# Other banks in the conv and pool stage, norm sums in mid-unit, and earlier splits of three weight units

## The chip, the cores and the metric

The kernel runs on one core of a Trainium2 chip. The metric is the device time of one execution in microseconds. A core has TensorE (matrix products, fp32 sums into eight PSUM banks), VectorE (DVE), ScalarE (ACT), GpSimd (POOL) and SyncE (SP), which issues the loads. The engines run their own instruction lists and meet only at semaphores.

## The reference

Two transformer-like blocks over 512 tokens of width 1024, all in fp32. The part around the change is the end of the first block (its feed-forward part between two RMS norms) and the first mixer of the second block, which runs a causal convolution of 31 taps on half of the channels and window means on the other half:

```
def hybrid_layer(x, ...):
    ...
    x = x + rms_norm(mix, g_post_mix)                     # norm 1
    h = rms_norm(x, g_pre_ffn)                            # norm 2
    f = jnp.square(jax.nn.relu(h @ w_ff1)) @ w_ff2
    return x + rms_norm(f, g_post_ffn)                    # norm 3

def conv_pool_mixer(h, w_in, dw_w, dw_b, ln_g, ln_b, pool_w, pool_scale, w_out):
    z = h @ w_in                                          # h = rmsnorm(x): norm 4
    a_val, a_gate, u = z[..., :512], z[..., 512:1024], z[..., 1024:]
    a = a_val * jax.nn.sigmoid(a_gate)
    a = causal_depthwise_conv(a, dw_w, 31 taps) + dw_b
    a = jax.nn.silu(layernorm(a, ln_g, ln_b))
    ...
    d = window_mean(u, (2, 4, 8, 16)) - u
    p = (d @ pool_w per group) * pool_scale
    return jnp.concatenate([a, p], axis=-1) @ w_out
```

## The kernel before

Activations lie transposed in SBUF: eight tiles of 128 channels by 512 tokens (`xT`, `acc`, `h_hi`/`h_lo`). Every big product is computed in three passes of a rounded high part and a low part: `h_hi*wlo`, `h_lo*whi`, `h_hi*whi`.

**Units.** Weights come in units of two k tiles by 512 columns. Each unit goes through four slots (`RING`): SyncE loads it into `raw`; ScalarE's `split` (L620 to L627) writes the rounded copy `whi`; POOL (L560, L571) subtracts and writes `wlo`; TensorE's `unit` (L1002 to L1026) does 24 products of 512 columns. `split(first, j)` handles unit `first + j + 2` and waits until TensorE has begun the unit three before it, so the slot is free. A group of four units fills four banks; its last unit either goes k tile by k tile, or (`by_tile`) finishes bank after bank.

**Banks.** `bank_plan` (L117 to L150) gives each use of a PSUM bank in a stage a number, and the waits on `filled` and `drained` follow from that table. The order of work on each engine is the order of the program text of that engine; no planner moves anything.

**A norm.** ScalarE squares each tile (`square`, L633), VectorE adds the squares into `ss` (`sum_square`, L1505 and L1508), TensorE multiplies `ss` by `ones` (`norm_sum`, L1053), ScalarE makes `rs` by a logarithm and an exponential (`inv_rms`, L638 and L641, "the root"). At norms 1 and 3, `post_normed` on VectorE then makes, per tile, `acc` (L1529), the new `xT` (L1532), and after ScalarE's `h_hi` (L651) the low part `h_lo` (L1496), and adds the squares of the next norm. Meanwhile TensorE keeps itself busy with small products (`keep_clock`, L1046) and starts the next group as tiles come. ScalarE splits the third and the fourth unit of that group ahead of tiles 3 and 5 (the `units` argument of `h_parts`). Norms 2 and 4 are summed behind the group's last unit.

**The conv and pool stage.** Twelve input units: group 0 (gates and values of conv tiles 0 and 1), group 2 (the pool channels `u`), group 1 (conv tiles 2 and 3). VectorE empties the banks: `gate_in` (L1807, into `csig`), `value_in` (L1813, into `apad`), `pool_in` (L1826, into `upad`), and `gated` (L1820) multiplies by the sigmoid. In between it runs the taps of conv tiles 0 and 1 (`tap`, L1842, in place in a PSUM bank), with the four `pool_in` after taps 9 to 12 and the emptying of group 1 at taps 24 to 29; then conv tile 2 in two banks, `even` and `odds` (L1886). TensorE does conv tile 3 with diagonal matrices (`conv_taps`, L1295), with four pool products (L1291) in the middle. Then come the output units, with the mean (L1320) after the first and the sum for the variance (L1325) after the second. For that sum ScalarE squares the four centred tiles (L859) and VectorE adds them (L1608).

The input groups stood in banks 0 to 3 all three times, the pool products too, and the taps in 4 to 6:

```
b.stage("cpin", [(("g", g, m), m) for g in (0, 2, 1) for m in range(4)] + [(("pool", j), j) for j in range(4)]
        + [(("taps", j), 4 + j) for j in range(3)] + [("odd", 4), ("mean", 5), ("conv", 7), ("var", 7)])
```

## Time and profile before

| what | value |
|---|---|
| median of 3 runs | 1880.56 us (1879.99 to 1881.3) |
| the profiled execution | 1879.24 us, its span 1877.5 us |
| TensorE products, busy | 1815.7 us, 97% of the span |
| VectorE busy | 840.3 us, 45% |
| ScalarE busy | 617.1 us, 33% |
| POOL busy | 723.3 us, 39% |
| mean granted TensorE clock | 0.992 |

All times below are microseconds from the span's start. In the timeline a row gives start, length, engine, line, operation, output and inputs, how many instructions, and in brackets how long the engine stood idle before it and what ended that. A product of 512 columns is recorded at 0.39 us but the next starts 0.23 us after it, since products overlap; a plain fp32 product has two records. Norm 1 lies near 275, the FFN from 282 to 640, norm 3 near 643, the conv and pool stage from 650 to 825.

### The profile page before, as it was taken

To read this page: it belongs to the slowest core of one execution; us is meant where nothing else is said; L and a number is where in the kernel's file an instruction comes from. 1 tells how busy PE (TensorE), PEld (TensorE's weight loads), DVE (VectorE), ACT (ScalarE), POOL (GpSimd) and SP (SyncE) were. 2 spreads that over 40 slices of the span, in tenths; PEclk is the share of its full clock that TensorE was granted. 3 is DMA by queue.
4 is the path that set the end of the run, shared out by engine and by line. 5 is a ranking of instruction groups with operands and counts; after the bars stand their busy time and mean duration, and the time that the engine had idled before them with its cause. 6 is when DMAs were issued, how large, how long until landed. Compare 5 with 4: busy or idle time off the path is not lost.

```text
span 1877.5 us, 24072 instructions
## 1 busy us (share of the span) xinstructions
PE 1815.7 (97%) x8442; PEld 1477.3 (79%) x8442; DVE 840.3 (45%) x1392; ACT 617.1 (33%) x814; POOL 723.3 (39%) x315
## 2 busy tenths in 40 slices
PE   8899989999999989999999999999999999999998
PEld 6688777888888765688888888888888788888886
DVE  2544436333333488533223244567566332232425
ACT  5444434222222332442222233343342342222323
POOL 3122224444444348243434443332232344344441
PEclk9999999999999999999999999999999999999999
DMA  8711112322332131132323223222121133232231
GB/s 199 124 57 56 57 56 84 96 89 90 101 101 99 59 106 46 56 99 81 112 89 101 93 85 101 68 68 67 45 78 56 56 102 112 89 101 93 85 102 45
DMA packets 149493, 159.78 MB, mean 85 GB/s; under 512 B 9891, under 2 KB 110871, under 8 KB 149439
## 3 DMA queue, kind: packets, MB, share of 16 engines
q1 hardware_dynamic: 148911, 158.79, 28.4%
q8 instruction: 34, 0.56, 0.1%
q10 hardware_dynamic: 528, 0.26, 0.0%
q14 instruction: 20, 0.16, 0.0%
HBM read 156.40 MB, written 2.62 MB: 85 GB/s over the span
## 4 chain that ended last, share of the span: by engine, by line
PE 52%; issue 30%; POOL 11%; DVE 4%; ACT 2%; DMA 0%; POOLq 0%; SPq 0%; DVEq 0%; ACTq 0%
PE ps L1020 46%; POOL wlo L560 10%; PE ps L1169 1%; PE ps L1295 1%; PE ps L1158 1%; DVE ss L1508 1%; DVE acc L1529 0%; DVE ps L1842 0%; PE ps L1133 0%; PE ps L1134 0%; DVE h_lo L1496 0%; POOL wlo L571 0%; DMA raw<-in_w_in 0%; PE ps L1053 0%; ACT whi L627 0%
## 5 line engine op out<-in xcount | busy, mean ns | idle before, releaser
L560 POOL TENSOR_TENSOR wlo<-raw,whi 128x1024 fp32r<-128x1024 f32 x272 | 658.0, 2432 | 1074.9 <-ACT whi L627 1060.5
L1020 PE MATMUL ps<-h_hi,wlo 128*128 128x512 f32 x1472 | 589.1, 400 | 13.9 <-DVE h_lo L1496 4.8
L1020 PE MATMUL ps<-h_hi,whi 128*128 128x512 f32 x1472 | 576.0, 391 | 0.0
L1020 PE MATMUL ps<-h_lo,whi 128*128 128x512 f32 x1472 | 574.9, 391 | 0.0
L627 ACT ACTIVATE whi<-raw 128x1024 fp32r<-128x1024 f32 x282 | 292.2, 1054 | 516.2 <-PE ps L1020 497.7
L1020 PEld LDWEIGHTS ps<-h_hi,wlo 128*128 128x128 f32 x1472 | 277.3, 188 | 76.7 <-issue 11.3
L1020 PE MATMUL ps<-m_hi,wlo 128*128 128x512 f32 x800 | 321.4, 402 | 3.2 <-DVE m_lo L1659 1.6
L1020 PEld LDWEIGHTS ps<-h_hi,whi 128*128 128x128 f32 x1472 | 276.9, 188 | 59.3
L1020 PEld LDWEIGHTS ps<-h_lo,whi 128*128 128x128 f32 x1472 | 277.3, 188 | 57.7 <-issue 2.9
L1020 PE MATMUL ps<-m_hi,whi 128*128 128x512 f32 x800 | 318.0, 397 | 0.0
L1020 PE MATMUL ps<-m_lo,whi 128*128 128x512 f32 x800 | 317.9, 397 | 0.0
L1936 DVE TENSOR_TENSOR gate<-ps,rs 128x512 f32<-128x512 f32 x44 | 30.4, 692 | 374.1 <-PE ps L1020 374.1
L1020 PEld LDWEIGHTS ps<-m_hi,wlo 128*128 128x128 f32 x800 | 151.3, 189 | 41.4 <-DVE m_lo L1659 2.0
L1020 PEld LDWEIGHTS ps<-m_lo,whi 128*128 128x128 f32 x800 | 151.2, 189 | 36.8 <-issue 1.2
L1020 PEld LDWEIGHTS ps<-m_hi,whi 128*128 128x128 f32 x800 | 151.1, 189 | 36.7
L1954 DVE TENSOR_TENSOR xT<-xT,ps 128x512 f32<-128x512 f32 x176 | 117.2, 685 | 68.5 <-PE ps L1020 68.5
L892 ACT ACTIVATE silu<-gate 128x512 f32<-128x512 f32 x44 | 27.8, 633 | 171.0 <-DVE gate L1936 171.0
L1753 DVE SCALAR_TENSOR_TENSOR relu<-ps,rs 128x512 f32<-128x512 f32 x32 | 21.9, 687 | 118.9 <-PE ps L1020 113.4
L1779 DVE TENSOR_TENSOR acc<-acc,ps 128x512 f32<-128x512 f32 x56 | 38.5, 688 | 80.1 <-PE ps L1020 79.9
L1394 PEld LDWEIGHTS ps<-qd,kk 128*128 128x128 f32 x448 | 56.9, 191 | 14.8 <-issue 9.6
L1394 PE MATMUL ps<-qd,kk 128*128 128x64 f32 x448 | 57.4, 271 | 6.7 <-DVE qd L2050 6.7
L571 POOL TENSOR_TENSOR wlo<-raw,whi 128x1024 fp32r<-128x1024 f32 x12 | 30.0, 2512 | 44.0 <-ACT whi L627 43.9
(240 smaller groups left out, 1404.7 us busy)
## 6 DMA issues: line engine op xcount, KB each, us to landing
raw<-in_ffn_w SPq DMA_DIRECT2D x264, 256.0 KB, 2.9
raw<-in_w_ff SPq DMA_DIRECT2D x128, 256.0 KB, 2.9
raw<-in_hg_w_in SPq DMA_DIRECT2D x64, 256.0 KB, 3.2
raw<-in_w_in SPq DMA_DIRECT2D x40, 256.0 KB, 5.5
raw<-in_cp_w_in SPq DMA_DIRECT2D x24, 256.0 KB, 2.9
raw<-in_w_out SPq DMA_DIRECT2D x16, 256.0 KB, 2.8
raw<-in_cp_w_out SPq DMA_DIRECT2D x16, 256.0 KB, 2.8
raw<-in_hg_w_out SPq DMA_DIRECT2D x16, 256.0 KB, 2.9
```

What stands on the lines that cost most here:

```text
L560: pool.tensor_tensor(wlo[:, u % RING, :, :], raw[:, u % RING, :, :], whi[:, u % RING, :, :].bitcast(F32), ALU.subtract).then_inc(unit_lo, 1)
L571: pool.tensor_tensor(wlo[:, u % RING, :, :], raw[:, u % RING, :, :], whi[:, u % RING, :, :].bitcast(F32), ALU.subtract).then_inc(unit_lo, 1)
L627: act.activation(whi[:, u % RING, :, :], raw[:, u % RING, :, :], ACT.Copy).then_inc(unit_hi, 1)
L892: act.activation(silu[:, i, :], gate[:, i, :], ACT.Silu).then_inc(silu_ready, 1)
L1020: mm = pe.matmul(ps[:, b, :], wt[:, s, a, m * P:(m + 1) * P], xt[:, kts[a], :], start=starts and a == 0 and i == 0, stop=last)
L1158: mm = pe.transpose(ps[:, 6, k * P:(k + 1) * P], prob[:, i % 2, k * P:(k + 1) * P], ident[:, :])
L1169: mm = pe.matmul(ps[:, 7, cols], probT[:, i % 2, k * P:(k + 1) * P], vtok[:, k * P + HEAD_DIM * e:k * P + HEAD_DIM * (e + 1)], start=k == ...
L1394: mm = pe.matmul(ps[:, b, t * 64:(t + 1) * 64], kk[:, t * P:(t + 1) * P], levels(qd[:, t * P:(t + 1) * P], m)[:, :, 1, :], start=True, sto ...
L1753: dve.scalar_tensor_tensor(out=relu[:, m % 2, :], in0=ps[:, b, :], scalar=0.0, in1=rs[:, :], op0=ALU.max, op1=ALU.mult).then_inc(drained[b ...
L1779: dve.tensor_tensor(acc[:, k, :], acc[:, k, :], ps[:, 4 + m, :], ALU.add)\
L1936: dve.tensor_tensor(gate[:, i, :], ps[:, i, :], rs[:, :], ALU.mult).then_inc(drained[i], 1)
L1954: dve.tensor_tensor(xT[:, k, :], xT[:, k, :], ps[:, 4 + m, :], ALU.add).then_inc(drained[4 + m], 1)
```

## The change

Five edits:

1. In the table, group 2 moves to banks 4 to 7, group 1 to banks 4, 3, 5, 2 (for m = 0 to 3; TensorE fills m in the order 3, 1, 2, 0), the taps to banks 0, 1 and 6, and the pool products to 0, 2, 3 and 5.
2. The third unit's split moves from ahead of tile 3 to ahead of the root, at norms 1 and 3.
3. At norms 1 and 3 VectorE no longer adds the eighth square: TensorE sums `ss` (seven squares) and then the eighth square itself in a second product into the same bank. `post_normed` counts `sq_used` on in its stead.
4. Norms 2 and 4 are summed in the middle of the group's last unit, between its first and second k tile (`halfway`), not behind it.
5. The split of the fifth output unit moves ahead of the four squares of the layer norm.

```
-    b.stage("cpin", [(("g", g, m), m) for g in (0, 2, 1) for m in range(4)] + [(("pool", j), j) for j in range(4)]
-            + [(("taps", j), 4 + j) for j in range(3)] + [("odd", 4), ("mean", 5), ("conv", 7), ("var", 7)])
+    b.stage("cpin", [(("g", 0, m), m) for m in range(4)] + [(("g", 2, m), 4 + m) for m in range(4)]
+            + [(("g", 1, m), (4, 3, 5, 2)[m]) for m in range(4)] + [(("taps", j), (0, 1, 6)[j]) for j in range(3)]
+            + [("odd", 4)] + [(("pool", j), (0, 2, 3, 5)[j]) for j in range(4)]
+            + [("mean", 5), ("conv", 7), ("var", 7)])
...
             wout_squares(second_half)
+            split(U_FFN, 0)
             inv_rms(1)
-            h_parts(1, 2, x_is(0), "g_pre_ffn", 0, {3: (U_FFN, 0), 5: (U_FFN, 1)})
+            h_parts(1, 2, x_is(0), "g_pre_ffn", 0, {5: (U_FFN, 1)})
...
             acc_squares(second_half)
+            split(U_CPIN, 0)
             inv_rms(3)
-            h_parts(2, 4, x_is(KT), "norm_mix_g_2", 0, {3: (U_CPIN, 0), 5: (U_CPIN, 1)})
+            h_parts(2, 4, x_is(KT), "norm_mix_g_2", 0, {5: (U_CPIN, 1)})
...
             split(U_CPOUT, 1)
+            split(U_CPOUT, 2)
             for j in range(4):
                 act.wait_ge(cln_step, j + 1)
                 act.activation(csq[:, j, :], conv[:, j, :], ACT.Square).then_inc(cln_sq, 1)
-            split(U_CPOUT, 2)
...
-                    unit(first, j0 + j, h_hi, h_lo, (2 * j, 2 * j + 1), stage, tags, j == 0, j == 3, turn, per, order,
-                         use, tile if n is not None else None, j == 3 and n is None)
+                    for part in (slice(0, 4), slice(4, 8)) if j == 3 and halfway else (slice(0, 8),):
+                        unit(first, j0 + j, h_hi, h_lo, (2 * j, 2 * j + 1), stage, tags, j == 0, j == 3, turn, per, order,
+                             use, tile if n is not None else None, j == 3 and n is None, part)
+                        if halfway and part.stop == 4:
+                            halfway()
...
-                pe.wait_ge(sq_used, KT * i)
-                pe.matmul(ps[:, b, :], ones[:, :], ss[:, :], start=True, stop=True).then_inc(filled[b], 1)
+                if i in (1, 3):
+                    pe.wait_ge(sq_used, KT * i - 1)
+                    pe.matmul(ps[:, b, :], ones[:, :], ss[:, :], start=True, stop=False)
+                    pe.wait_ge(sq_ready, KT * i)
+                    pe.matmul(ps[:, b, :], ones[:, :], sq[:, (KT - 1) % 2, :], start=False, stop=True).then_inc(filled[b], 1)
+                else:
+                    pe.wait_ge(sq_used, KT * i)
+                    pe.matmul(ps[:, b, :], ones[:, :], ss[:, :], start=True, stop=True).then_inc(filled[b], 1)
...
-            group(U_FFN, 0, "ffn0", up_tags, n=1, between=norm_after(2, 3))
+            group(U_FFN, 0, "ffn0", up_tags, n=1, halfway=lambda: norm_sum(2))
...
-            group(U_CPIN, 0, "cpin", [("g", 0, m) for m in range(4)], order=(2, 3, 0, 1), n=2, between=norm_after(4, 3))
+            group(U_CPIN, 0, "cpin", [("g", 0, m) for m in range(4)], order=(2, 3, 0, 1), n=2,
+                  halfway=lambda: norm_sum(4))
...
                 dve.wait_ge(rs_ready, rs_n)
+                dve.sem_inc(sq_used, 1)
...
-                if k % 4 == 3:
+                if k == 3:
                     sum_square(1, k)
...
-                    if last:
-                        sum_square(3, 4 * h + 3)
+                    if last and h == 0:
+                        sum_square(3, 3)
```

ScalarE's list from the last squares of norm 3 to tile 3, before (`sq<-acc` squares of norm 3, `rs` the root, `whi` a split):

```order
200 L633 ACTIVATE sq<-acc 128x512 x4
201 L638 ACTIVATE rs<-ps,eps6 128x512
202 L641 ACTIVATE rs<-rs 128x512
203 L651 ACTIVATE h_hi<-xT,vecs 128x512
204 L633 ACTIVATE sq<-xT 128x512
205 L651 ACTIVATE h_hi<-xT,vecs 128x512
206 L633 ACTIVATE sq<-xT 128x512
207 L651 ACTIVATE h_hi<-xT,vecs 128x512
208 L633 ACTIVATE sq<-xT 128x512
209 L627 ACTIVATE whi<-raw 128x1024
210 L651 ACTIVATE h_hi<-xT,vecs 128x512
```

and in the change:

```order
200 L635 ACTIVATE sq<-acc 128x512 x4
201 L629 ACTIVATE whi<-raw 128x1024
202 L640 ACTIVATE rs<-ps,eps6 128x512
203 L643 ACTIVATE rs<-rs 128x512
204 L653 ACTIVATE h_hi<-xT,vecs 128x512
205 L635 ACTIVATE sq<-xT 128x512
206 L653 ACTIVATE h_hi<-xT,vecs 128x512
207 L635 ACTIVATE sq<-xT 128x512
208 L653 ACTIVATE h_hi<-xT,vecs 128x512
209 L635 ACTIVATE sq<-xT 128x512
210 L653 ACTIVATE h_hi<-xT,vecs 128x512
```

The split moved from row 209 to row 201, ahead of both steps of the root; the same happened at norm 1.

TensorE's list around the sum of norm 3 and the small products that follow it, before:

```order
1530 L1020 MATMUL ps<-m_lo,whi 128x512
1531 L1020 MATMUL ps<-m_hi,whi 128x512
1532 L1053 MATMUL ps<-ss,ones 128x512
1533 L1046 MATMUL ps<-ident 128x128 x20
1534 L1020 MATMUL ps<-h_hi,wlo 128x512
```

and in the change:

```order
1531 L1024 MATMUL ps<-m_lo,whi 128x512
1532 L1024 MATMUL ps<-m_hi,whi 128x512
1533 L1062 MATMUL ps<-ss,ones 128x512
1534 L1064 MATMUL ps<-sq,ones 128x512
1535 L1054 MATMUL ps<-ident 128x128 x20
1536 L1024 MATMUL ps<-h_hi,wlo 128x512
```

One plain fp32 product was added, reading the eighth square directly. The sum of norm 4 (L1067 in the change) moved from row 1630, behind the last unit of group 0, to row 1620, with twelve of that unit's products behind it.

ScalarE's list at the layer norm of the conv stage (`late` the squares, `crs` its root), before:

```order
238 L851 ACT_TABLE_LOAD
239 L854 ACTIVATE conv<-ps,vecs 128x512
240 L627 ACTIVATE whi<-raw 128x1024
241 L859 ACTIVATE late<-conv 128x512 x4
242 L627 ACTIVATE whi<-raw 128x1024
243 L862 ACTIVATE crs<-ps,eps6 128x512
```

and in the change:

```order
238 L855 ACT_TABLE_LOAD
239 L858 ACTIVATE conv<-ps,vecs 128x512
240 L629 ACTIVATE whi<-raw 128x1024 x2
241 L864 ACTIVATE late<-conv 128x512 x4
242 L866 ACTIVATE crs<-ps,eps6 128x512
```

The second split now stands ahead of the four squares.

## Rows read from the trace of the kernel before

**Rows 1.** The page, busy us (share of the span) and instructions of TensorE.

```profile
PE   1815.7 (97%) x8442; PEld 1477.3 (79%) x8442; DVE 840.3 (45%) x1392; ACT 617.1 (33%) x814; POOL 723.3 (39%) x315
```

**Rows 2.** TensorE's waits by releaser: us in total, times, longest us.

```profile
PE ps L1020 <- DVE h_lo L1496: 4.8, 4, 1.7
...
PE ps L1053 <- DVE ss L1508: 4.5, 2, 2.3
```

**Rows 3.** Timeline, norm 1: start us, length us, engine, line, operation, [idle before].

```profile
274.02 1.48 DVE L1508 TENSOR_TENSOR ss<-ss,sq 128x512 f32<-128x512 f32 x2
275.64 1.10 PE L1053 MATMUL ps<-ss,ones 128*128 128x512 f32 x2 [2.27 <-DVE ss L1508]
...
276.78 0.69 ACT L638 ACTIVATE rs<-ps,eps 128x512 f32<-128x512 f32 x1 [2.01 <-PE ps L1053]
...
278.16 0.75 DVE L1529 SCALAR_TENSOR_TENSOR acc<-acc,vecs,rs 128x512 f32<-128x512 f32 x1 [2.66 <-ACT rs L641]
```

**Rows 4.** Timeline, the tiles behind norm 1, four engines.

```profile
286.97 1.04 ACT L627 ACTIVATE whi<-raw 128x1024 fp32r<-128x1024 f32 x1
...
288.09 2.39 POOL L560 TENSOR_TENSOR wlo<-raw,whi 128x1024 fp32r<-128x1024 f32 x1 [22.09 <-ACT whi L627]
...
288.66 2.37 DVE L1496 SCALAR_TENSOR_TENSOR h_lo<-xT,vecs,h_hi 128x512 fp32r<-128x512 f32 x1 [0.88 <-ACT h_hi L651]
...
293.60 2.88 DVE L1508 TENSOR_TENSOR ss<-ss,sq 128x512 f32<-128x512 f32 x1
...
298.58 0.50 PE L1020 MATMUL ps<-h_hi,wlo 128*128 128x512 f32 x1 [1.74 <-DVE h_lo L1496]
```

**Rows 5.** Timeline of TensorE, norm 3 and the tiles behind it.

```profile
642.77 1.61 PE L1053 MATMUL ps<-ss,ones 128*128 128x512 f32 x2 [2.27 <-DVE ss L1508]
...
666.23 0.50 PE L1020 MATMUL ps<-h_hi,wlo 128*128 128x512 f32 x1 [1.71 <-DVE h_lo L1496]
```

**Rows 6.** Windows: us, TensorE busy (instructions), granted clock, DMA share, GB/s.

```profile
644.00:646.00 2.00, 2.00 (x10) 0.50 0.00 0
...
678.00:680.00 2.00, 0.94 (x4) 1.00 0.50 172
...
706.00:708.00 2.00, 2.00 (x6) 0.50 0.00 0
```

**Rows 7.** Timeline, the three input groups of the conv and pool stage.

```profile
677.03 1.29 DVE L1807 TENSOR_TENSOR csig<-ps,rs 128x512 f32<-128x512 f32 x2 [5.34 <-ACT rs L641]
...
679.06 0.47 PE L1020 MATMUL ps<-h_hi,wlo 128*128 128x512 f32 x1 [3.51 <-DVE apad L1813]
...
682.97 11.94 DVE L1842 SCALAR_TENSOR_TENSOR ps<-apad,taps,ps 128x512 f32<-128x512 f32 x18
...
697.07 0.69 DVE L1826 TENSOR_TENSOR upad<-ps,rs 128x512 f32<-128x512 f32 x1 [2.16 <-PE ps L1020]
...
700.72 0.39 PE L1020 MATMUL ps<-h_hi,whi 128*128 128x512 f32 x1
...
703.65 0.47 PE L1020 MATMUL ps<-h_hi,wlo 128*128 128x512 f32 x1 [2.54 <-DVE upad L1826]
```

**Rows 8.** Timeline, the end of group 1 and the conv taps.

```profile
723.28 0.69 DVE L1807 TENSOR_TENSOR csig<-ps,rs 128x512 f32<-128x512 f32 x1 [5.28 <-PE ps L1020]
...
729.86 13.97 PE L1295 MATMUL ps<-apad,late 128*128 128x512 f32 x32 [2.54 <-DVE apad L1820]
```

**Rows 9.** Timeline, squares and sum of the conv stage's layer norm.

```profile
767.39 2.43 ACT L859 ACTIVATE late<-conv 128x512 f32<-128x512 f32 x4 [5.57 <-DVE conv L1906]
...
769.72 1.04 ACT L627 ACTIVATE whi<-raw 128x1024 fp32r<-128x1024 f32 x1
770.16 3.60 DVE L1608 TENSOR_TENSOR csum<-csum,late 128x512 f32<-128x512 f32 x2
770.84 2.37 POOL L571 TENSOR_TENSOR wlo<-raw,whi 128x1024 fp32r<-128x1024 f32 x1 [6.26 <-ACT whi L627]
...
773.90 1.10 PE L1325 MATMUL ps<-csum,ones 128*128 128x512 f32 x2 [1.66 <-DVE csum L1608]
```

3 lines of the change are left out of this document (2 added, 1 removed).

## The prediction

> **What bounds the kernel now.** I read the page first: TensorE counts as busy for 97% of the span [rows 1], so only stretches in which it stands still, or runs below full clock, can give time back. Next come TensorE's waits, sorted by who ended them. The largest that this change can reach are on `h_lo`, 4.8 us in four waits, and on the norm sums, 4.5 us in two [rows 2]. Then I walked the timeline through the places that the diff touches. No TensorE wait is listed between 300 and 640 us, nor between 800 and 1200 us, so what is won at a norm or in the conv stage is not given back behind it: later work shifts as a block. The pace of the block: group 2 is 96 products of 512 columns, 95 steps from 679.06 to 700.72 us, 0.228 us each [rows 7], so a unit of 24 takes 5.47 us. A plain fp32 product (a sum against `ones`, a conv tap) holds TensorE 0.87 us: 13.97 us for 16 taps of two records [rows 8]. A VectorE operation in a row of others takes 0.66 us (11.94 us for 18) [rows 7].
>
> **Step 1, the two-part sums of norms 1 and 3.** Before, VectorE makes its last two adds from 274.02 on (1.48 us) and TensorE's sum starts at 275.64 [rows 3]. Now seven squares are enough: they are added at 274.7, TensorE starts at 274.84, and its second product follows 0.87 us later at 275.71, against 275.64. The extra product eats the add that it saves. Value 0 (-0.1 to +0.1). At norm 3 the sum took 1.61 us in place of 1.10 [rows 3, 5], and the granted clock was 0.50 right behind it [rows 6]. TensorE now stands still 0.8 us less ahead of it; I count 0.4 us there (0 to 0.5).
>
> **Step 2, the third unit's split ahead of the root.** Before, the split takes ScalarE 1.04 us at 286.97, ahead of `h_hi` 3; VectorE's `h_lo` 3 comes 0.88 us late for it, and then lasts 2.37 us in place of 0.74, till POOL's product of the same unit (288.09, 2.39 us) is done [rows 4]. Loss on VectorE: 0.88 + 1.63 = 2.5 us. Now ScalarE splits from 274.8 to 275.9, inside the 2.01 us that it waits for the sum anyway [rows 3], and POOL's product runs from about 275.95 to 278.35, where VectorE has nothing to do until 278.16. Behind that product all of `post_normed` is queued (eight each of `acc`, `xT`, `h_lo`, and the adds); it can be 0 to 0.25 us late. The fourth unit's split stays, and with it the add of 2.88 us at 293.60 [rows 4]. What is late next: `h_lo` 5 was done 20.4 us after the first `acc` and is now done after 17.9. TensorE starts 3.5 us after the first `acc` (five VectorE operations) and wants tile 5 after 60 products, 13.7 us later, so at 17.2: it still waits, some 0.6 us. Norm 1: **2.4 us** (2.2 to 2.6), of the 1.74 us in [rows 4] and 0.9 at `h_lo` 3. Norm 3, where the last such wait is 1.71 us and ends at 666.23 [rows 5], with the 0.4 of step 1: **2.9 us** (2.2 to 3.1).
>
> That an operation with two SBUF inputs stands for the whole of POOL's product is what the row of 2.37 us shows. The Trainium skill, SBUF — State Buffer, Who interferes with whom, has it as a lock: VectorE with two SBUF inputs and a GpSimd operation exclude one another for a whole instruction, and who issues first wins. By that rule the moved product still holds the first `acc` till 278.35, and would hold it 2.4 us if it began just before 278.16; with its start at 275.95 the sum is the same by rule and by row.
>
> **Step 3, norm sums in mid-unit.** Norm 2: TensorE does the same products in another order, VectorE has its `rs` some 2.7 us earlier, and nobody on the path waited for it. Value 0; down to -0.3 if the last add misses the half (it stands eight operations, 5.3 us, behind `h_lo` 5; TensorE's half point 24 products, 5.5 us). Norm 4: before, VectorE's first `csig` came at 677.03 after 5.34 us of idleness [rows 7]. The sum now comes 12 products, 2.7 us, earlier, on top of the 2.9 us, so `rs` is there near 671.4 and the taps of tiles 0 and 1 begin 5.5 us earlier. That alone gives nothing; it is what step 4 needs.
>
> **Step 4, the banks.** (a) Before, group 2 began in bank 0, which `value_in` empties: TensorE waited 3.51 us till 679.06 [rows 7]. Now tile 5 is taken at 663.3, 36 products and the sum bring group 2 to 672.5, and it begins in bank 4, emptied by the logarithm of the norm near 671. The low parts of its first two units are done near 671 and 673.3; the second is wanted at 678. Gain **3.5 us**. (b) Before, group 1 began in bank 3 and waited 2.54 us for the last `upad`, till 703.65 [rows 7]. Now its first banks, 2 and 3, were emptied by `csig` 20 us earlier; then come 5 and 4, emptied by `upad` 1 and 0. `upad` 0 waits for the first tile of group 2's last unit, 18.0 us into the group (679.06 to 697.07, [rows 7]): 690.5. `upad` 1 is three operations later and done at 693.2. Group 1 starts at 672.5 + 21.9 = 694.4 and wants bank 5 at 695.8: 2.6 us to spare. Gain **2.5 us**. (c) Behind that wait the clock reads 0.50 from 706 to 708 us [rows 6], and group 1 needs 19.6 us to the same point of its last unit (703.65 to 723.28, [rows 7, 8]) where group 2 needed 18.0. Without the fall **1.6 us** go as well. Nothing in these rows says that a gap must bring it: the 3.51 us ahead of 679.06 left the clock at 1.00 [rows 6]. (d) The taps in banks 0, 1 and 6 are the same operations of 0.66 us; 0, as no row shows a pace that hangs on the bank.
>
> **Step 5, what is late next in the conv stage.** The conv taps wait for `apad` 3, made 6.58 us after VectorE's `csig` (723.28 to 729.86, [rows 8]). That `csig` wants the first tile of the last unit: 694.4 + 18.0 = 712.4. VectorE gets there 32 operations after 690.5: 711.6. So TensorE is still the one waited for, but by 0.8 us, where it was 5.28 us. The conv taps start at 719.0, 2.6 us after group 1 ends. By the parts this is 2.9 + 3.5 + 2.5 + 1.6 = 10.5 us earlier, by the walk 10.9; I take 10.5. From the `csig` on, VectorE needs 53 operations, 35 us, for its own conv tiles, and TensorE 6.58 + 35 products of 0.87 us (31 taps, 4 pool products) + ScalarE's 0.7 = 37.8 us: TensorE keeps the bound. POOL's three products for the output units begin about 11 us behind that `csig`, before 9.5; they may hold one add for 1 us inside the 2.8 us. The pool products' banks 0, 2, 3 and 5 are free over 5 us before their use.
>
> **Step 6, the split ahead of the squares.** It waits until TensorE begins the second output unit, about 0.5 us before the first square could start (767.39, [rows 9]). The four squares queued behind it start 0.58 us later, and VectorE's adds wait for them. Before, POOL's product (770.84, 2.37 us) held the last add: two adds took 3.60 us, and TensorE waited 1.66 us till 773.90 [rows 9]. Now the product runs from 768.05 to 770.45 and holds the first add; the three end at 771.0, 771.6 and 772.3, and the sum starts at 772.45. **Gain 1.4 us** (0.9 to 1.8).
>
> **The sum.** 2.4 + 2.9 + 3.5 + 2.5 + 1.6 + 1.4 = 14.3 us. The profiled execution took 1879.24 us around a span of 1877.5, so it becomes 1864.9; the median of the runs shown lies 1.3 us higher: 1866.3 us.
>
> **Rivals.**
> - *One more fall of the clock.* The gap ahead of the conv taps is as long as the one that ended at 703.65. If the clock falls there, about 1.6 us come back: 1867.9. Against it: the same gap at 729.86 left the taps at 0.87 us. Chance 0.28.
> - *VectorE becomes the bound.* Only 0.8 us lie between its arrival and TensorE's tile. If POOL holds two of its operations or `upad` 0 comes late, 1 to 2 us: 1867.8. Chance 0.12.
> - *The norms give nothing.* POOL's moved product starts late and stands in front of `acc`, so that another wait takes the place of the 5.3 us: 1871.6. For it: the fourth unit's product still holds an add 2.2 us. Chance 0.07.
> - *The banks don't free TensorE.* Bank 5 or 4 is empty only after 695.8; the wait and the fall behind it return, 4.1 us: 1870.4. Needs `upad` 1 later by 2.6 us. Chance 0.04.
> - *Slower.* The clock falls ahead of the conv taps and stays down through all 35 fp32 products: 30.5 us double, 1866.3 + 30.5 = 1896.8. It decides from 14.3 us of such work on. For it, the two low stretches in [rows 6]; against, both had group work running through them at full pace a few us later. Chance 0.02.
>
> **How the numbers follow.** The forecast as worked out has 0.47. A measurement of this kernel can tell about 0.2%, 3.8 us; all cases but the last lie beyond it. I leave 0.03 for no measurable change and 0.02 for slower, so 0.95 for faster. The range goes down 2.3 us for the upper bounds of the gains (0.2, 0.2, 0.4 by step 5's walk, 0.4) and the spread of the runs (0.7), and up to the first, second and fourth rival: 1864.0 to 1870.6. The norms' rival, the slow one and the 0.03 stay outside.
>
> **What would show it.** The `h_lo` waits of TensorE fall from 4.8 us to about 1; POOL's product ends before the first `acc` at both roots; no wait on `apad` behind norm 4's sum, none on `upad`; the clock at 1.00 in group 1; the gap ahead of the conv taps still there; the wait at the variance sum falls from 1.7 to 0.4. Wrong, if the last `csig` finds its bank long filled, if a low clock appears in the conv taps, or if a POOL product stands across an `h_lo` of tile 3 as before.

## The result, and the profile after

The changed kernel took 1866.47 us (median of four runs, 1865.42 to 1868.81), the kernel before, beside it, 1880.93 us (four runs, 1879.99 to 1882.42): a ratio of 0.9929, 95% interval 0.9914 to 0.9943. The forecast was 1866.3 us. The profiled execution of the changed kernel is the slowest of its four: 1868.81 us around a span of 1867.0 us, 2.3 us above its median. Four executions recorded further on fell into a slow state (2867.19 us of e1, 3024.97 of e3, 3669.31 of e4, and 7368.95 of the kernel before beside them), and all medians and ratios here leave them out.

All segments below are differences of start times in the two timelines. TensorE's last product before norm 1 starts at 272.98 us before and at 275.02 us after: 2.04 us were lost there before any edit matters, to stretches of low clock at 48 to 56 and 242 to 252 us that lasted longer than in the kernel before. From that product to the last one before norm 3 it is 367.13 us before and 364.52 after (2.61 gained), from there to the variance sum of the conv stage 133.79 and 125.59 (8.20 gained), from there to the end 1103.6 and 1101.9 (1.7 gained; before has a low clock at 1462 to 1466 us and after has none there). -2.0 + 2.6 + 8.2 + 1.7 is the 10.5 us between the two spans.

TensorE's waits in the changed kernel, by releaser (us in total, times, longest us), against [rows 2]:

```profile
PE ps L1310 <- DVE apad L1836: 4.1, 1, 4.1
...
PE ps L1062 <- DVE ss L1523: 2.9, 2, 1.5
...
PE ps L1024 <- DVE h_lo L1511: 0.7, 2, 0.4
...
PE ps L1340 <- DVE csum L1624: 0.6, 1, 0.6
```

The wait on `h_lo` fell from 4.8 to 0.7 us, and the waits for banks that held `apad` and `upad` are gone from L1024 altogether. But the conv taps (L1310) wait 4.1 us for `apad`, where it was 2.5.

Norm 1 and the tiles behind it, timeline of the changed kernel (as [rows 3, 4]):

```profile
277.83 2.35 POOL L562 TENSOR_TENSOR wlo<-raw,whi 128x1024 fp32r<-128x1024 f32 x1 [9.79 <-ACT whi L629]
...
280.40 0.75 DVE L1545 SCALAR_TENSOR_TENSOR acc<-acc,vecs,rs 128x512 f32<-128x512 f32 x1 [3.65 <-ACT rs L643]
...
289.94 0.75 DVE L1511 SCALAR_TENSOR_TENSOR h_lo<-xT,vecs,h_hi 128x512 fp32r<-128x512 f32 x1
...
293.26 2.88 DVE L1523 TENSOR_TENSOR ss<-ss,sq 128x512 f32<-128x512 f32 x1
```

POOL's product of the third unit ends at 280.18, 0.2 us before VectorE's first `acc`, so it holds nobody; at norm 3 it ends at 644.70, again 0.2 us before the first `acc` at 644.92. `h_lo` of tile 3 takes 0.75 us (2.37 before, behind 0.88 us of idleness). The fourth unit's product still holds an add of squares for 2.88 us, as it did.

Norm 3, timeline of TensorE (as [rows 5]) and the window around it (us, busy, instructions, granted clock, DMA share, GB/s):

```profile
641.41 1.10 PE L1062 MATMUL ps<-ss,ones 128*128 128x512 f32 x2 [1.47 <-DVE ss L1523]
642.34 1.02 PE L1064 MATMUL ps<-sq,ones 128*128 128x512 f32 x2
...
662.78 0.50 PE L1024 MATMUL ps<-h_hi,wlo 128*128 128x512 f32 x1 [0.36 <-DVE h_lo L1511]
```

```profile
638.00:646.00 8.00, 6.53 (x39) 1.00 0.12 36
```

The sum runs at full clock, and the clock stays full behind it, where [rows 6] had 0.50.

The conv stage, timeline of VectorE, POOL and TensorE (as [rows 7, 8]):

```profile
667.70 7.35 POOL L562 TENSOR_TENSOR wlo<-raw,whi 128x1024 fp32r<-128x1024 f32 x3 [7.58 <-ACT whi L629]
...
670.88 1.29 DVE L1823 TENSOR_TENSOR csig<-ps,rs 128x512 f32<-128x512 f32 x2 [2.63 <-ACT rs L643]
672.09 1.28 DVE L1829 TENSOR_TENSOR apad<-ps,rs 128x512 f32<-128x512 f32 x2
...
673.79 4.62 DVE L1836 TENSOR_TENSOR apad<-apad,csig 128x512 f32<-128x512 f32 x2 [0.43 <-ACT csig L833]
...
675.23 2.62 POOL L562 TENSOR_TENSOR wlo<-raw,whi 128x1024 fp32r<-128x1024 f32 x1 [0.18 <-ACT whi L629]
...
679.88 11.94 DVE L1858 SCALAR_TENSOR_TENSOR ps<-apad,taps,ps 128x512 f32<-128x512 f32 x18
...
712.55 0.68 DVE L1823 TENSOR_TENSOR csig<-ps,rs 128x512 f32<-128x512 f32 x1
...
719.76 16.40 PE L1310 MATMUL ps<-apad,late 128*128 128x512 f32 x32 [4.08 <-DVE apad L1836]
```

Two gated products (L1836, `apad` by `csig`) that need 1.3 us alone take 4.62; in the kernel before they took 1.56:

```profile
679.94 1.56 DVE L1820 TENSOR_TENSOR apad<-apad,csig 128x512 f32<-128x512 f32 x2 [0.43 <-ACT csig L829]
```

In the changed kernel they stand behind POOL's row of `wlo` products. The four operations ahead of them (L1823 and L1829), which take one of their inputs from PSUM (`ps`), lie inside the same row and are not held: 1.29 and 1.28 us for two. The third `csig`, at 712.55, has no wait in front of it: VectorE comes to a bank that is already filled (0.93 us before, as b1 will show), where it waited 5.28 us in the kernel before. And the 32 records of the first 16 conv taps take 16.40 us, not 13.97. The windows say why (columns as above):

```profile
694.00:710.00 16.00, 16.00 (x72) 1.00 0.16 59
...
718.00:720.00 2.00, 0.24 (x1) 0.50 0.00 0
720.00:722.00 2.00, 2.00 (x3) 0.50 0.00 0
722.00:724.00 2.00, 2.00 (x3) 0.50 0.01 4
724.00:726.00 2.00, 2.00 (x5) 0.84 0.00 0
```

Group 1 now runs at full clock. The fall that stood behind the `upad` wait has moved behind the `apad` wait, into fp32 products.

The layer norm's squares and sum in the changed kernel (as [rows 9]):

```profile
760.43 2.41 POOL L573 TENSOR_TENSOR wlo<-raw,whi 128x1024 fp32r<-128x1024 f32 x1 [3.52 <-ACT whi L629]
761.71 1.68 DVE L1624 TENSOR_TENSOR csum<-late 128x512 f32<-128x512 f32 x1 [0.22 <-DVE conv L1922]
...
763.50 1.49 DVE L1624 TENSOR_TENSOR csum<-csum,late 128x512 f32<-128x512 f32 x2
765.13 1.10 PE L1340 MATMUL ps<-csum,ones 128*128 128x512 f32 x2 [0.55 <-DVE csum L1624]
```

POOL's product holds the first add and not the last two, and the wait ahead of the sum is 0.55 us in place of 1.66.

### The profile page after: what moved, and what is told of

Same layout as the page of the kernel before. It is cut to its first block, busy times and chain, and to the rows that moved or that the text cites. A ratio compares the mean times of both kernels' runs of the same rounds, so it can differ in the third digit from the quotient of the medians.

```text
span 1867.0 us, 24060 instructions
## 1 busy us (share of the span) xinstructions
PE 1814.0 (97%) x8446; PEld 1475.3 (79%) x8446; DVE 840.3 (45%) x1390; ACT 616.9 (33%) x814; POOL 722.3 (39%) x315
## 4 chain that ended last, share of the span: by engine, by line
PE 50%; issue 30%; POOL 11%; DVE 6%; ACT 2%; DMA 0%; POOLq 0%; SPq 0%; DVEq 0%; ACTq 0%
PE ps L1024 44%; POOL wlo L562 10%; DVE ps L1858 2%; PE ps L1310 2%; PE ps L1183 1%; PE ps L1172 1%; DVE ss L1523 1%; DVE acc L1545 1%; PE ps L1147 0%; PE ps L1148 0%; DVE h_lo L1511 0%; POOL wlo L573 0%; DVE xT L1548 0%; DMA raw<-in_w_in 0%; ACT L742 0%
## 5 line engine op out<-in xcount | busy, mean ns | idle before, releaser
L1024 PE MATMUL ps<-h_hi,wlo 128*128 128x512 f32 x1472 | 588.5, 400 | 5.1 <-POOL wlo L562 1.6
L1024 PE MATMUL ps<-h_hi,whi 128*128 128x512 f32 x1472 | 575.3, 391 | 0.0
L1024 PE MATMUL ps<-h_lo,whi 128*128 128x512 f32 x1472 | 574.2, 390 | 0.0
L1024 PEld LDWEIGHTS ps<-h_hi,wlo 128*128 128x128 f32 x1472 | 277.0, 188 | 66.1 <-issue 5.3
L1024 PE MATMUL ps<-m_hi,wlo 128*128 128x512 f32 x800 | 321.7, 402 | 3.3 <-DVE m_lo L1675 1.6
L1024 PEld LDWEIGHTS ps<-h_hi,whi 128*128 128x128 f32 x1472 | 276.5, 188 | 59.0
L1024 PEld LDWEIGHTS ps<-h_lo,whi 128*128 128x128 f32 x1472 | 277.0, 188 | 58.0 <-issue 3.1
L1024 PE MATMUL ps<-m_lo,whi 128*128 128x512 f32 x800 | 318.0, 398 | 0.0
L1024 PE MATMUL ps<-m_hi,whi 128*128 128x512 f32 x800 | 318.0, 398 | 0.0
L1024 PEld LDWEIGHTS ps<-m_hi,wlo 128*128 128x128 f32 x800 | 151.3, 189 | 41.4 <-DVE m_lo L1675 2.0
L1024 PEld LDWEIGHTS ps<-m_lo,whi 128*128 128x128 f32 x800 | 151.4, 189 | 36.8 <-issue 1.2
L1024 PEld LDWEIGHTS ps<-m_hi,whi 128*128 128x128 f32 x800 | 151.2, 189 | 36.8
```

Source lines behind the costliest of these rows:

```text
L1024: mm = pe.matmul(ps[:, b, :], wt[:, s, a, m * P:(m + 1) * P], xt[:, kts[a], :], start=starts and a == 0 and i == 0, stop=last)
```

## The experiments

The theory to be tested: each edit gives about what the prediction's list says, and the 3.9 us that the conv stage falls short of it in the profile (1.5 in the wait, 2.4 in the taps) have one root, GpSimd's `wlo` products in front of VectorE's gated products, and one follower, the clock. The rivals: that the gap belongs to the chain from `csig` to `apad` however early VectorE is, and that the fall of the clock is chance. Each kernel ran beside the kernel before; e1 to e5 are the kernel before with one of the five edits, the others start from the changed kernel. Segments are of the one profiled execution of each, from TensorE's last product before norm 1 (N1) or norm 3 (N3); "tile 5" is the first product that waits for `h_lo` of tile 5, and "16 taps" is the length of the row of the first 16 conv taps:

| kernel | N1 to N3 | N3 to tile 5 | wait, bank 0 or 4 | wait, `upad` | N3 to conv taps | wait there | 16 taps | N3 to variance sum |
|---|---|---|---|---|---|---|---|---|
| before | 367.13 | 26.12 | 3.51 | 2.54 | 89.75 | 2.54 | 13.97 | 133.79 |
| changed | 364.52 | 23.24 | 0 | 0 | 80.22 | 4.08 | 16.40 | 125.59 |
| changed, again | 364.52 | 23.24 | 0 | 0 | 80.19 | 4.05 | 16.42 | 125.58 |
| banks alone (e1) | 368.08 | 26.07 | 0.87 | 0 | 82.85 | 2.73 | 13.97 | 126.90 |
| splits alone (e2) | 364.50 | 23.71 | 3.51 | 2.54 | 87.47 | 2.72 | 15.67 | 133.22 |
| mid-unit sums alone (e3) | 366.94 | 26.18 | 0.74 | 3.28 | 88.00 | 2.97 | 15.67 | 133.73 |
| two-part sums alone (e4) | 367.26 | 25.81 | 3.51 | 2.54 | 90.83 | 2.67 | 13.97 | 134.88 |
| output split alone (e5) | 368.02 | 26.15 | 3.51 | 2.54 | 89.75 | 2.54 | 13.97 | 132.68 |
| changed, old banks (e6) | 364.49 | 23.22 | 0.76 | 3.30 | 84.86 | 2.54 | 13.97 | 127.81 |
| changed, late split (b1) | 364.54 | 23.23 | 0 | 0 | 78.84 | 2.72 | 15.67 | 123.48 |
| changed, early pool products (b2) | 364.53 | 23.23 | 0 | 0 | 80.22 | 2.34 | 13.97 | 121.44 |
| changed, filler products (b4) | 364.53 | 23.22 | 0 | 0 | 80.11 | 1.72 | 14.00 | 123.07 |
| changed, b1 and b2 and filler (b3) | 364.55 | 23.23 | 0 | 0 | 78.73 | 0.23 | 14.01 | 120.19 |
| changed, late split, early gate (b5) | 364.55 | 23.23 | 0 | 0 | 75.97 | 0 | 13.90 | 119.03 |

Where the clock does the same, a segment repeats to some 0.05 us between executions, which is why the edits are read from segments. Whole runs of one kernel spread over 0.5 us (b4) to 8 us (e5), mostly over 2.5 to 5.

### One edit at a time

**The banks (e1).** Only the new bank table of the `cpin` stage:

```diff
-    b.stage("cpin", [(("g", g, m), m) for g in (0, 2, 1) for m in range(4)] + [(("pool", j), j) for j in range(4)]
-            + [(("taps", j), 4 + j) for j in range(3)] + [("odd", 4), ("mean", 5), ("conv", 7), ("var", 7)])
+    b.stage("cpin", [(("g", 0, m), m) for m in range(4)] + [(("g", 2, m), 4 + m) for m in range(4)]
+            + [(("g", 1, m), (4, 3, 5, 2)[m]) for m in range(4)] + [(("taps", j), (0, 1, 6)[j]) for j in range(3)]
+            + [("odd", 4)] + [(("pool", j), (0, 2, 3, 5)[j]) for j in range(4)]
+            + [("mean", 5), ("conv", 7), ("var", 7)])
```

> The kernel before with the new bank table of the cpin stage and nothing else. My theory (the price list of the prediction, but with the sum of norm 4 still behind the first input group): TensorE no longer waits for apad and upad; it still waits in bank 4 for the logarithm of norm 4, some 0.9 us of the 3.5, so 2.6 + 2.5 us are gained, and 1.6 more where the clock then stays full: about -7 us, 1874. VectorE then has hardly any slack: the conv taps wait about as long as before. Rival (the cover of VectorE is used up, as the trace of after suggests): the conv taps' wait grows to 3 or 4 us, 1.5 less is gained, and the clock falls ahead of the conv taps, 1.6 to 2.4 less again: -3 to -4 us, 1877.

Measured: 1874.19 us, ratio 0.9964 (0.9950 to 0.9978). TensorE and VectorE in its timeline:

```profile
679.57 0.47 PE L1022 MATMUL ps<-h_hi,wlo 128*128 128x512 f32 x1 [0.87 <-ACT rs L640]
```

```profile
719.29 0.69 DVE L1809 TENSOR_TENSOR csig<-ps,rs 128x512 f32<-128x512 f32 x1 [0.38 <-PE ps L1022]
```

```profile
726.06 13.97 PE L1297 MATMUL ps<-apad,late 128*128 128x512 f32 x32 [2.73 <-DVE apad L1822]
```

The wait in bank 4 is the 0.87 us for the logarithm, the `upad` wait and the fall behind it are gone, and the conv taps start 6.90 us earlier from norm 3 on: the 7 us of the theory. VectorE's first gated products took 1.60 us here, since the sum of norm 4 is late and POOL's product ends at 683.53, 0.45 us into them; so VectorE came 0.38 us before TensorE's tile, and there was next to nothing to lose at the taps. In N1 to N3 this execution had a low clock behind norm 1 (276 to 282 us), which no edit of e1 touches, and it cost 0.95 us.

**The split ahead of the root (e2).**

```diff
+            split(U_FFN, 0)
             inv_rms(1)
-            h_parts(1, 2, x_is(0), "g_pre_ffn", 0, {3: (U_FFN, 0), 5: (U_FFN, 1)})
+            h_parts(1, 2, x_is(0), "g_pre_ffn", 0, {5: (U_FFN, 1)})
...
+            split(U_CPIN, 0)
             inv_rms(3)
```

> The kernel before with the third unit's split ahead of the root in norms 1 and 3 and nothing else. My theory: 2.4 us behind norm 1 and 2.5 behind norm 3, of which the wait in bank 0 of the conv stage takes nothing back, since the whole of the stage moves: -4.9 us, 1876. Rival (the split gives no time in one of the two places since a lock on VectorE's h_lo decides there, not the root): -2.5 us, 1878.4.

Measured: 1872.83 us, ratio 0.9963 (0.9949 to 0.9978). 2.63 us from norm 1 to norm 3 and 2.41 from norm 3 to tile 5, as the theory has it; the rival of one place alone is out. Of the 2.41 us, 2.28 reach the conv taps. There the clock fell and the taps took 15.67 us, so the profile shows only 0.57 us at the variance sum. The whole runs give 7.0 us (4.1 to 9.6 by the interval) where the two segments give 5.0; they can't tell the one from the other.

**The sums in mid-unit (e3).** Both calls of `group` with `halfway` in place of `between`, and the loop over two halves of its last unit:

```diff
-            group(U_FFN, 0, "ffn0", up_tags, n=1, between=norm_after(2, 3))
+            group(U_FFN, 0, "ffn0", up_tags, n=1, halfway=lambda: norm_sum(2))
```

> The kernel before with the sums of norms 2 and 4 in mid-unit and nothing else. My theory: nothing in the FFN; in the conv stage csig is some 5 us earlier, and the 3.5 us wait for bank 0 shrinks to about 0.9: -2.6 us, 1878.2, the upad wait and the fall of the clock may stay. Rival (the move has no effect without the banks): 0 us, 1880.9.

Measured: 1878.19 us, ratio 0.9988 (0.9978 to 0.9998). The wait in bank 0 fell from 3.51 to 0.74 us as expected, but the conv taps start only 1.75 us earlier, and as the clock then fell in them (15.67 us), nothing of it is left at the variance sum (133.73 against 133.79 us). The timelines of VectorE and TensorE show who took the rest:

```profile
676.28 4.54 DVE L1825 TENSOR_TENSOR apad<-apad,csig 128x512 f32<-128x512 f32 x2 [0.43 <-ACT csig L829]
```

```profile
700.71 0.76 PE L1020 MATMUL ps<-h_hi,wlo 128*128 128x512 f32 x1 [3.28 <-DVE upad L1831]
```

This is the first run that separates the edits on the point: the gated products take 1.55 to 1.60 us in e1 and e2 and 4.54 us here. It is the earlier sum of norm 4 that moves them into POOL's row: in this run POOL's row of three products lasts till 677.47 and a fourth follows at 677.73.

**The sums in two parts (e4).**

```diff
-                pe.wait_ge(sq_used, KT * i)
-                pe.matmul(ps[:, b, :], ones[:, :], ss[:, :], start=True, stop=True).then_inc(filled[b], 1)
+                if i in (1, 3):
+                    pe.wait_ge(sq_used, KT * i - 1)
+                    pe.matmul(ps[:, b, :], ones[:, :], ss[:, :], start=True, stop=False)
+                    pe.wait_ge(sq_ready, KT * i)
+                    pe.matmul(ps[:, b, :], ones[:, :], sq[:, (KT - 1) % 2, :], start=False, stop=True)
...
```

> The kernel before with the sums of norms 1 and 3 made of two products and nothing else. My theory: 0 us behind norm 1, 0.4 us behind norm 3, where VectorE's last addition goes and a product of 0.4 to 0.9 us comes: -0.4 us, 1880.4. Rival (the early first product keeps TensorE's clock full through the sum of norm 3): 0.5 to 0.8 us more, -1.1 us, 1879.8. Rival on the other side: the second product in fp32 costs as much as the addition saves, 0.

Measured: 1882.23 us, ratio 1.0002 (0.9992 to 1.0012). Behind norm 1 nothing (367.26 against 367.13 us), behind norm 3 0.31 us (25.81 against 26.12). The first of the two sum products of norm 3 in e4, and the one sum product in e2:

```profile
644.17 1.10 PE L1054 MATMUL ps<-ss,ones 128*128 128x512 f32 x2 [1.47 <-DVE ss L1514]
```

```profile
640.41 1.77 PE L1055 MATMUL ps<-ss,ones 128*128 128x512 f32 x2 [2.27 <-DVE ss L1510]
```

All five kernels with the sum in one part show the clock fall at norm 3 (their sum takes 1.56 to 1.77 us in place of 1.10), and two of them (e1, e5) also at norm 1, where it cost 0.9 us. None of the nine profiles with the sum in two parts shows it in either place. So the rival of the fuller clock is right in its mechanism, and the clock is all of the gain: at full clock, behind norm 1, TensorE reaches tile 5 after 25.60 us with the one-part sum (before) and after 25.81 us with the two-part sum (e4), which is 0.2 us lost. Behind norm 3 the fall turns the 25.60 us into 26.12, and e4 has 25.81 again: 0.5 us of clock less 0.2 us of edit is the 0.31. Whether the shorter wait or the added product keeps the clock was not separated. The profile of e4 is slower from norm 3 to the conv taps (90.83 us) because the clock fell behind the 3.51 us wait in bank 0, at 680 to 688 us: from the start of group 2 to that of group 1 it is 27.47 us, where the kernel before has 24.59. e4 changes nothing there.

**The split ahead of the squares (e5).**

```diff
             split(U_CPOUT, 1)
+            split(U_CPOUT, 2)
             for j in range(4):
                 act.wait_ge(cln_step, j + 1)
                 act.activation(csq[:, j, :], conv[:, j, :], ACT.Square).then_inc(cln_sq, 1)
-            split(U_CPOUT, 2)
```

> The kernel before with the split of the third output unit ahead of the conv squares and nothing else. My theory (step 6 of the prediction): the wait ahead of the variance sum falls from 1.66 to 0.4 or 0.6 us: -1.1 to -1.4 us, 1879.6. Rival (the first units' later products take it back): 0, 1880.9.

Measured: 1877.8 us, ratio 0.9987 (0.9977 to 0.9996); the wait ahead of the variance sum is 0.56 us in place of 1.66, and the sum comes 1.11 us earlier from norm 3 on (132.68 against 133.79):

```profile
774.79 1.10 PE L1325 MATMUL ps<-csum,ones 128*128 128x512 f32 x2 [0.56 <-DVE csum L1608]
```

**The changed kernel without the banks (e6).** The old bank table in the changed kernel.

> The changed kernel with the bank table of before. My theory (with the sum of norm 4 in mid-unit and the split ahead of the root, the old table costs 0.9 us in bank 0 and 2.5 us or more at upad, and the clock falls behind that wait): group 1 ends 3.4 to 5 us later. TensorE's tile is then late and VectorE is ready for it, so the conv taps wait 2.6 us and not 4.1, which gives 1.5 us back: 2 to 3.5 us slower than the changed kernel, 1869 to 1870. Rival (the prices of the prediction hold as they are, 3.5 and 2.5 and 1.6 us): 7.6 us slower, 1874.

Measured: 1868.23 us, ratio 0.9941 (0.9926 to 0.9957), where the changed kernel beside it has 0.9925 (0.9911 to 0.9939).

```profile
695.08 0.47 PE L1022 MATMUL ps<-h_hi,wlo 128*128 128x512 f32 x1 [3.30 <-DVE upad L1840]
```

The old table costs 0.76 us in bank 0, 3.30 at `upad`, and a fall of the clock behind that. The taps start 4.64 us later from norm 3 on than with the new table, and wait 2.54 us. But then the clock stays full in the taps, so that at the variance sum 2.22 us are left of the 4.64. The rival, that the prices of the prediction are worth 7.6 us in company too, is out for the profiles: alone the banks gave 6.9 us at the taps, with the other edits 4.6, and 2.2 at the variance sum, since without them the clock stayed full in the taps. The intervals of the two ratios overlap, so the whole runs can't tell what the banks are worth in company.

### Where the 3.9 us went

**The late split (b1).** In the changed kernel, ScalarE's split of input unit 4 goes from between the root of norm 4 and the two sigmoids to behind them:

```diff
             inv_rms(4)
-            split(U_CPIN, 4)
...
             sigmoid_of(0, 0)
             sigmoid_of(0, 1)
-            for j in range(5, 12):
+            for j in range(4, 12):
                 split(U_CPIN, j)
```

> The changed kernel with the split of input unit 4 behind the two sigmoids of csig. Theory A (VectorE's first gated product was held by GpSimd's wlo products, and VectorE is then late all the way to the conv taps): the first gated product takes 1.6 us a piece again, VectorE's taps start some 2 to 3 us earlier, the conv taps wait 2.6 us and not 4.1 us: -1.5 us against the changed kernel, 1865, and up to 2.4 more if the clock then stays full in the conv taps. Theory B (VectorE's own work between group 2 and apad decides, however early it starts): the wait stays at 4.1 us, 0 us. On the other side: unit 4's wlo comes late for its own products, a new wait at the head of group 2 of 1 to 2 us, slower by that.

Measured: 1864.66 us, ratio 0.9919 (0.9903 to 0.9936). VectorE's and TensorE's timelines:

```profile
669.51 1.28 DVE L1835 TENSOR_TENSOR apad<-apad,csig 128x512 f32<-128x512 f32 x2
...
672.27 11.94 DVE L1857 SCALAR_TENSOR_TENSOR ps<-apad,taps,ps 128x512 f32<-128x512 f32 x18
...
707.87 0.69 DVE L1822 TENSOR_TENSOR csig<-ps,rs 128x512 f32<-128x512 f32 x1 [0.84 <-PE ps L1023]
```

```profile
714.63 15.67 PE L1309 MATMUL ps<-apad,late 128*128 128x512 f32 x32 [2.72 <-DVE apad L1835]
```

Theory A holds: the gated products take 1.28 us, VectorE's row of 18 taps starts 36.48 us behind norm 3's last product and not 40.34, 3.86 us earlier. Of that 3.34 us are the gated products (4.62 against 1.28); the other 0.5 us are the sigmoids, which are there sooner because the split no longer stands ahead of them. VectorE waits again for TensorE's tile (0.84 us), and the conv taps start 1.38 us earlier. That the 3.9 us on VectorE bring 1.4 and not 3.9 is TensorE's tile: VectorE, waiting for it, takes it 72.08 us behind N3 (b1 and b5 alike). The changed kernel's `csig` at 712.55 stands 73.01 behind, 0.93 us late, and its next gated product is held again (1.31 us against 0.86), 0.45 more. Those two are the 1.4. No new wait came at the head of group 2. The clock still fell, for a shorter time: the taps took 15.67 us.

**The early pool products (b2).** In the changed kernel, pool products 1 and 2 are issued ahead of the wait for `apad`, and 0 and 3 stay behind the first 16 taps:

```diff
+            pe.wait_ge(poolw_in, 16)
+            pool_product(1)
+            pool_product(2)
...
             pe.wait_ge(apad_ready, 3)
             conv_taps(0, 16)
-            pe.wait_ge(poolw_in, 16)
-            for j in range(4):
-                pool_product(j)
+            pool_product(0)
+            pool_product(3)
```

> The changed kernel with pool products 1 and 2 ahead of the conv taps, in TensorE's wait for apad. Theory A (the gap of 4.1 us is idle and the fall of the clock comes from it): two products of 0.9 us move into the gap, -1.7 us, and the conv taps run at full clock, -2.4 us more in those executions where it fell: 1863 to 1865. Theory B (the chain on VectorE's side, not TensorE's, sets the end of the stage): the time moves to the wait behind the conv taps or ahead of the first output unit, 0 us.

Measured: 1863.26 us, ratio 0.9905 (0.9888 to 0.9921).

```profile
719.45 13.97 PE L1310 MATMUL ps<-apad,late 128*128 128x512 f32 x32 [2.34 <-DVE apad L1838]
```

The taps start at the same point, 80.22 us behind N3, and the 1.72 us of the two products are gone behind them. The clock stays at 1.00, which is 2.43 us more: together the variance sum comes 4.15 us earlier. Theory B is out; nobody behind the taps took it back.

**Filler products (b4).** In the changed kernel ten products that nothing uses, from the kernel's own `keep_clock`, stand ahead of the wait for `apad`:

```diff
             pe.wait_ge(tapdiag_ready, 1)
+            keep_clock(7, 10)
             pe.wait_ge(apad_ready, 3)
```

> The changed kernel with ten small products that nothing uses (those of the kernel's own helper that fills waits) in the wait for apad. Theory A (the idle gap ahead of the conv taps is what lowers the clock): granted clock 1.00 all through the conv taps, which take 14.0 us and not 16.4; -2.4 us where the clock fell, so up to -2.4 in the median, 1864 to 1866. Theory B (the fall comes from something else): the clock is 0.50 at the taps as before, 0 us.

Measured: 1865.93 us, ratio 0.9922 (0.9906 to 0.9939); the taps start where they did (80.11 us), at full clock:

```profile
719.06 14.00 PE L1310 MATMUL ps<-apad,late 128*128 128x512 f32 x32 [1.72 <-DVE apad L1837]
```

As far as single profiles can say, the fall follows TensorE's idleness in this gap: it came in both profiles of the changed kernel, and in none of the four in which the gap was filled or gone (b2, b4, b3, b5). In the profiles the fillers give 2.5 us at the variance sum; in the medians they give little that can be told: the ratio is 0.9922 against 0.9929 and 0.9925 for the changed kernel. The four runs of b4 lie within 0.5 us (1865.81 to 1866.33), the nine of the changed kernel within 3.9 (1864.94 to 1868.84).

**The changed kernel again (after_copy).**

> The changed kernel itself, on the chip of the next three. Theory A (the wait of 4.1 us for apad and a fall of the clock behind it belong to this kernel): both come again, the conv taps take 15.7 to 16.4 us at a granted clock of 0.5 to 0.8, 1866.5. Theory B (the fall of the clock there was chance): the same wait of 4.1 us and 14.0 us for the taps.

Measured: 1867.68 us, ratio 0.9925 (0.9911 to 0.9939). The profile repeats the first: 4.05 us of waiting and 16.42 us for the taps, with the clock at 0.50 from 718 to 724 us. Its five runs fall into two kinds, 1864.94 and 1864.99 us with a mean clock of 0.995 to 0.996, and 1867.68, 1868.57 and 1868.84 us with 0.993. Both profiles are of the second kind. A fall such as this one takes 0.002 off the mean clock (some 7 us at half of it), so the two kinds are what one fall more or less would make; but the records of the runs without a profile don't say where a fall was, so this stays a reading, not a finding.

**Both, and filler (b3_all).** b1 and b2 together, with three filler products behind them.

> The changed kernel with the split of input unit 4 behind the two sigmoids, pool products 1 and 2 ahead of the conv taps, and three small products that nothing uses behind them. Theory A (the gains of the single edits are of different things and add up): the conv taps' wait is 1 us or less, the clock stays full, -1.4, -1.7 and 0 to -2.4 us against the changed kernel: 1862. Theory B (both edits fill the same gap): no better than the pool products alone, 1863.3.

Measured: 1862.65 us, ratio 0.9898 (0.9883 to 0.9914). The wait is 0.23 us, the clock full, and the variance sum comes 5.40 us earlier than in the changed kernel (120.19 against 125.59): 1.4 + 1.7 + 2.4 is 5.5. The gains add up in the profile, and b2's alone is exceeded by 1.25 us. The filler's share is not separated: b2 kept the clock without it.

**The early gate (b5).** b1, and in VectorE's program the gated product of tile 1 in group 1 two tap pairs earlier:

```diff
                 if i == 25:
                     value_in(1, 1)
+                    gated(1, 1, 3)
                 if i == 26:
                     gate_in(1, 0)
                 if i == 27:
-                    gated(1, 1, 3)
                     value_in(1, 0)
```

> The changed kernel with the split of input unit 4 behind the two sigmoids and VectorE's gated product of value tile 1 two tap pairs earlier (at tap 25, not 27). Theory A (the 2.7 us that the conv taps still waited with the late split are VectorE's program order, not TensorE's tile): apad is there when TensorE ends its last input unit, the wait is 0 to 0.3 us, the clock stays full, and the variance sum comes 4 us earlier than with the late split alone: 1860 to 1861. Theory B (the gated product then waits for a sigmoid, or is held by GpSimd): the wait shrinks to 1 to 2 us only, 1863. On the other side: VectorE's sum for the mean, 3.3 us ahead of its product with the late split alone, becomes the next wait and takes up to 1 us back.

Measured: 1861.85 us (1861.32 to 1862.07), ratio 0.9899 (0.9884 to 0.9914). VectorE and TensorE in its timeline:

```profile
714.06 0.69 DVE L1835 TENSOR_TENSOR apad<-apad,csig 128x512 f32<-128x512 f32 x1
```

```profile
715.31 13.90 PE L1309 MATMUL ps<-apad,late 128*128 128x512 f32 x32
```

There is no wait ahead of the conv taps, and the clock is 1.00 from 714 to 722 us. Against b1 the taps start 2.87 us earlier and the variance sum comes 4.45 us earlier. So the 2.5 to 2.7 us that the taps waited even where VectorE was on time was no property of the data: `apad` was made three tap pairs after its `csig`, by an order written out in the kernel. The side effect that was named is there as well. Timeline of VectorE, POOL and TensorE at the mean's sum:

```profile
747.31 2.91 DVE L1912 TENSOR_TENSOR csum<-csum,conv 128x512 f32<-128x512 f32 x1
...
750.25 0.69 DVE L1917 TENSOR_TENSOR csum<-csum,conv 128x512 f32<-128x512 f32 x1
```

```profile
747.27 2.40 POOL L573 TENSOR_TENSOR wlo<-raw,whi 128x1024 fp32r<-128x1024 f32 x1 [10.77 <-ACT whi L629]
```

```profile
751.09 1.10 PE L1334 MATMUL ps<-csum,ones 128*128 128x512 f32 x2
```

POOL begins 0.04 us ahead of VectorE's add, which then takes 2.91 us; the add behind it is done at 750.94, 0.15 us ahead of the product that reads the sum. The slack of 3.3 us that b1 had there is used up. A further gain ahead of this point would have to move that split too.

b5 and b3_all beat the changed kernel too: beside them on the same chip its ratio is 0.9925 and its fastest run 1864.94 us, while their slowest are 1862.07 and 1864.26 us. Between the two no difference can be told.

## Why the prediction was right, and where it wasn't

**Step 1 (0 and 0.4 us)** holds in its sizes: 0.1 us lost and 0.31 gained in e4. The 0.31 is wholly the clock, which the two-part sum left full in all nine profiles; at full clock the edit costs 0.2 us.

**Step 2 (2.4 and 2.9 us)** holds: 2.63 alone and 2.61 with the rest at norm 1, 2.41 alone and 2.88 with step 1 at norm 3. The mechanism is the one named. The wait left at tile 5 was put at 0.6 us and is 0.35. That a VectorE operation with two SBUF inputs and a POOL product exclude each other for a whole instruction, and that the first to begin wins (the Trainium skill, SBUF — State Buffer, Who interferes with whom), is borne out at both ends: POOL's product ends 0.2 us ahead of the first `acc` at norm 1 and costs nothing, and one that began 0.04 us ahead of an add held it for 2.91 us in b5.

**Step 3** holds in its first half (the norm 2 sum costs nothing: 366.94 us against 367.13 in e3; `csig` 5.6 us earlier: 31.34 us behind N3 against 36.92). It fails in its second: "the taps of tiles 0 and 1 begin 5.5 us earlier". They began 2.5 us earlier (the row of 18 at 40.34 us behind N3 against 42.86). The missing 3.06 us are the two gated products, 4.62 us in place of 1.56. The step moved VectorE's two gated products and didn't ask what POOL does at the new place. The rule just cited was applied at the norms and forgotten here, though [rows 4] shows the case. b1 takes POOL's product away, and the two take 1.28 us. "That alone gives nothing" was wrong as well: alone (e3) the earlier sum took 2.77 us off the wait in bank 0 and brought the conv taps 1.75 us forward.

**Step 4 (3.5 + 2.5 + 1.6 us)** holds: 8.19 us from norm 3's last product to that of group 1 behind step 2's 2.88 (86.82 against 75.75 us), against 7.6. The bank waits are gone, the fall behind `upad` too. About half of the 0.6 us more is that an idle time as listed isn't the whole delay: from start to start the two waits delayed TensorE by 3.65 us (674.54 to 679.06, less the 0.87 of the sum) and 2.70 us (700.72 to 703.65, less one step), not 3.51 and 2.54. As a single edit the banks are worth 6.9 us. But the whole wait in bank 0 isn't theirs, as the step has it: the banks alone remove most of it (0.87 us left in e1), and so does the mid-unit sum alone (0.74 left in e3).

**Step 5 (VectorE 0.8 us before TensorE's tile, a gap of 2.6 us)** is where the failure of step 3 comes out. VectorE came 0.93 us after the tile. The gap is 4.08 us: the rival "VectorE becomes the bound", priced at 1 to 2 us and given 0.12. It cost 1.4 to 1.5 us, by just the cause that it names: POOL held two operations. Then the longer gap was followed by a fall of the clock, the rival "one more fall of the clock", priced at 1.6 and given 0.28. It cost 2.43 us in both profiles of the changed kernel. I had treated the two as separate cases. The profiles speak for a link, without proving it: of the unfilled gaps ahead of the taps those of 2.5 to 2.7 us were followed by a fall in two of seven, those of 3.0 and 4.1 us in three of three. Two of the signs that the prediction names for being wrong, the `csig` that finds its bank filled and the low clock in the conv taps, both came. What spoke against the fall in the prediction, that "the same gap at 729.86 left the taps at 0.87 us", was true of one execution: in e2 and b1 a gap of 2.72 us was followed by a fall, in e1 one of 2.73 us and in e4 one of 2.67 us weren't.

**Step 6 (1.4 us)** is right in mechanism and 0.3 too large. In the clock of before, POOL's product and the first add end where they were put (770.5 and 771.1). But the two adds behind them take 1.49 us and start 0.11 late, where 1.3 was counted. They take what two adds in a row into `ss` took at norm 1, 1.48 us [rows 3].

**The sum.** In the profile the change gave 10.5 us of span, not 14.3: 3.9 less in the conv stage by step 5, 0.3 less by step 6, 0.6 more by step 4, 0.2 more by step 2, and -2.0 and +1.7 of clock falls elsewhere, which give 10.6. That the median of 1866.47 us lies 0.2 us from the forecast is therefore in part luck: the forecast went from profile to profile and added 1.3 us, and the profile of the changed kernel, at 1868.81 us, lies 3.9 us above the 1864.9 us that it gives. The conv stage gives less than the sum says in both profiles of the changed kernel, while falls of the clock that no step speaks of move a run by as much either way: its nine runs reach from 1864.94 to 1868.84 us, with 1866.63 in the middle. The range has a slip in its lower end: the terms listed for it add up to 1.9 us and not 2.3, so it should have begun at 1864.4 us, which changes nothing here.

What stays open: what decides, at one and the same gap, whether the clock falls. Behind 3.51 us in bank 0 it fell in e2 and e4 and not in before and e5; behind 2.54 us at `upad` it fell in before and e5 and not in e2 and e4; behind 4.05 and 4.08 us it fell both times. Each kernel has one profile (the changed one two), so this gives no rate. Apart from the banks no edit was taken out of the changed kernel, so what the others give in company is read from its segments. Nor was it tried to take the fourth unit's product off the add that it still holds for 2.88 us behind norms 1 and 3.
